# Expert weights in three steps: when a duo's gate, up and down transfers begin

## The reference

```
hid = silu(xe @ e_gate) * (xe @ e_up)      # e_gate, e_up: 1024 x 2816 each
ye  = hid @ e_down * gate                  # e_down: 2816 x 1024
```

## Time and profile before

| | us |
|---|---|
| median of 3 runs (3658.36 to 3662.4) | 3662.31 |
| profiled execution | 3664.57 |
| its span, first to last instruction | 3662.8 |
| TensorE busy (matmul rows) | 3345.7 (91%) |
| VectorE busy | 2133.3 (58%) |
| DMA: 670.98 MB over the span | 183 GB/s on average |

### The profile page before, as it was taken

One profiled execution on the slowest core, in us unless ns is written; L12 is line 12 of the kernel. 1 busy time (PEld: TensorE's weight loads), 2 busy tenths in 40 slices (PEclk: granted clock), 3 DMA queues, 4 the chain that ended last, 5 costly groups with the idle time before them and its releaser, 6 DMA issues.

```text
span 3662.8 us, 154096 instructions
## 1 busy us (share of the span) xinstructions
PE 3345.7 (91%) x72354; PEld 2883.5 (79%) x72354; DVE 2133.3 (58%) x3890; ACT 764.4 (21%) x1815; POOL 384.6 (10%) x536
## 2 busy tenths in 40 slices
PE   7989898998999986699999999999999999999998
PEld 3575767666555543599999999999999999999997
DVE  3567566665344445556566566565656565665655
ACT  3434344443344432000000000000000000000002
POOL 0142415243211000000000000000001000000001
PEclk9999999999999987799999999999999999999999
DMA  8200000000311131878778777777778777877775
GB/s 348 70 5 9 18 9 17 10 14 4 101 32 26 42 110 58 304 258 282 264 276 276 267 280 264 275 271 267 267 268 281 263 270 271 284 269 266 270 269 191
DMA packets 500361, 670.98 MB, mean 183 GB/s; under 512 B 31598, under 2 KB 438406, under 8 KB 496654
## 3 DMA queue, kind: packets, MB, share of 16 engines
q1 hardware_dynamic: 494030, 641.74, 49.8%
q0 software_dynamic: 5520, 19.34, 2.5%
q10 hardware_dynamic: 176, 0.05, 0.0%
HBM read 631.68 MB, written 28.30 MB: 180 GB/s over the span
## 4 chain that ended last, share of the span: by engine, by line
PE 56%; issue 3%; DVE 0%; DMA 0%; ACT 0%; DVEq 0%; POOLq 0%
PE banks L2508 34%; PE banks L2533 20%; PE banks L2449 2%; DMA e_xe<-scratch_h2d,idx 0%; DVE e_wgu L2812 0%; DVE e_wgu L2881 0%; DVE e_xe L2870 0%; DVE e_wsum L2720 0%; DVE e_wsum L2725 0%; DVE e_wgu L2715 0%; ACT e_xp L2648 0%; ACT e_xT L2648 0%; DVE e_wsum L2710 0%; DVE e_ye L2783 0%; DVE e_xpT L2729 0%
## 5 line engine op out<-in xcount | busy, mean ns | idle before, releaser
L2533 PE MATMUL banks<-e_hid,e_wd 128*64 128x144 f32 x11264 | 1273.1, 287 | 21.2 <-issue 18.1
L2533 PEld LDWEIGHTS banks<-e_hid,e_wd 128*64 128x64 f32 x11264 | 768.5, 137 | 32.9 <-issue 32.5
L2508 PE MATMUL banks<-e_xsum,e_wgu 128*64 128x72 f32 x11264 | 524.6, 227 | 32.2 <-issue 31.7
L2508 PE MATMUL banks<-e_xsum,e_wsum 128*64 128x72 f32 x11264 | 525.9, 227 | 25.9 <-issue 23.8
L2508 PEld LDWEIGHTS banks<-e_xsum,e_wgu 128*64 128x64 f32 x11264 | 499.4, 138 | 36.4 <-issue 35.8
L2508 PEld LDWEIGHTS banks<-e_xsum,e_wsum 128*64 128x64 f32 x11264 | 501.3, 137 | 31.3 <-issue 29.0
L2508 PE MATMUL banks<-e_xT,e_wgu 128*64 128x72 f32 x11264 | 515.5, 227 | 10.7 <-issue 10.5
L2743 DVE TENSOR_TENSOR e_gu<-e_first,banks 128x288 f32<-128x288 f32 x176 | 80.0, 455 | 762.3 <-ACT e_first L2629 565.3
L2508 PEld LDWEIGHTS banks<-e_xT,e_wgu 128*64 128x64 f32 x11264 | 496.6, 137 | 13.6 <-issue 13.6
L2629 ACT ACTIVATE e_first<-banks 128x144 f32<-128x144 f32 x176 | 51.1, 290 | 1518.7 <-PE banks L2508 1518.7
L2508 PE MATMUL banks<-e_xT,e_wsum 128*64 128x72 f32 x5632 | 263.0, 227 | 22.7 <-issue 22.3
(11 more groups left out here) (401 smaller groups left out, 4750.1 us busy)
## 6 DMA issues: line engine op xcount, KB each, us to landing
e_wgu<-in_e_gate SPq DMA_DIRECT2D x176, 1024.0 KB, 5.4
e_wgu<-in_e_up SPq DMA_DIRECT2D x176, 1024.0 KB, 8.7
e_wd<-in_e_down SPq DMA_DIRECT2D x176, 1024.0 KB
h_wmod<-in_w_mod SPq DMA_DIRECT2D x24, 1024.0 KB, 15.3
wblk<-in_w_in SPq DMA_DIRECT2D x22, 512.0 KB, 21.7
h_x<-in_x_sample SPq DMA_DIRECT2D x8, 512.0 KB, 6.9
wo<-in_w_out SPq DMA_DIRECT2D x2, 2048.0 KB, 12.0
scratch_ffn<-hT_x SPq DMA_DIRECT2D x8, 512.0 KB, 5.1
```

The source lines that it names most:

```text
L2508: last = nc.tensor.matmul(bank[4 + 2 * (n % 2) + g][c, q * HT:(q + 1) * HT], a[:, k, c], b[:, k, :], start=(k == 0), stop=(k == HALF - 1))
L2533: last = nc.tensor.matmul(bank[k // PER_BANK][c, at:at + TOK], wd[n % WD][:, b, k * P + h * CH:k * P + (h + 1) * CH], hid[n % 2][:, b, :], ...
```

## The change

A second semaphore, `products_done` (`pace` in the code), is raised by each of the first thirteen products of a duo; the fourteenth raises `gu_ps` as before. SyncE no longer waits on `gu_ps` in the loop. It begins the gate transfer of duo n after the first product of duo n - 3, the up transfer after the sixth, and the down transfer after the tenth (and, as before, after `used` allows it). The slots, sizes and order of the transfers stay, and the first four duos are loaded without waiting for the gate and up slots, as before.

```diff
--- before.py
+++ after.py
@@ -2303,7 +2303,7 @@
         bank = K.bank
         g_in = [sem(f"gate_up_in{i}") for i in range(WG)]
         d_in = [sem(f"down_in{i}") for i in range(WD)]
-        used = sem("duo_used")
+        used, pace = sem("duo_used"), sem("products_done")
         rows = sem("gt2_in")
         x_in, xh_ps, x_ps, xa_ok, xv_ok, xs_ok = (sem(n) for n in ("x_in", "xT_half_psum", "xT_psum", "xT_act", "xT_dve", "x_sums"))
         ts_ok, ws_ok, wsum_ok = sem("token_chain"), sem("weight_chain"), sem("weight_sums")
@@ -2355,9 +2355,13 @@
                     e, j = divmod(n, ND)
                     f = slice(j * DUO * P, (j + 1) * DUO * P)
                     if n >= WG:
-                        sp.wait_ge(gu_ps, n - WG + 1)
+                        sp.wait_ge(pace, (STEPS - 1) * (n - WG + 1) + 1)
                     sp.dma_start(wgu[n % WG][:, 0, :, :], gv[:, e, :, f]).then_inc(g_in[n % WG], 16)
+                    if n >= WG:
+                        sp.wait_ge(pace, (STEPS - 1) * (n - WG + 1) + 6)
                     sp.dma_start(wgu[n % WG][:, 1, :, :], uv[:, e, :, f]).then_inc(g_in[n % WG], 16)
+                    if n >= WG:
+                        sp.wait_ge(pace, (STEPS - 1) * (n - WG + 1) + 10)
                     if n >= WD:
                         sp.wait_ge(used, n - WD + 1)
                     sp.dma_start(wd[n % WD][:, :, :], dv[:, e, j * DUO:(j + 1) * DUO, :]).then_inc(d_in[n % WD], 16)
@@ -2594,13 +2598,13 @@
                             pe.wait_ge(wsum_ok, n + 1)
                         last = product(n, 0, q)
                         if mats(n) == 2:
+                            last.then_inc(pace, 1)
                             done = downs(done, STEPS * n + 2 * q)
                             last = product(n, 1, q)
                         else:
                             for i in range(2 * KD * q // QS, 2 * KD * (q + 1) // QS):
                                 last = up(n, i)
-                        if q == QS - 1:
-                            last.then_inc(gu_ps, 1)
+                        last.then_inc(gu_ps if q == QS - 1 else pace, 1)
                         done = downs(done, STEPS * n + 2 * q + 1)
                         if n and q == 3:
                             between(*divmod(n - 1, ND))
```

## The result

| | before | after |
|---|---|---|
| median of 4 runs each | 3660.34 us | 3577.72 us (3574.02 to 3581.53) |
| ratio | | 0.9776, 95% interval 0.9759 to 0.9793 |
| profiled execution | 3664.57 us | 3574.02 us |
| its span | 3662.8 us | 3572.3 us |

The change makes the kernel 2.2% faster. The prediction said 3629 us, 0.9%, with a range from 3588: the direction and the bound hold, the gain is two and a half times as large.

A forecast was written before the change was run, and what follows sets the result against it. TensorE bounds the kernel, idle 0.765 us per duo at block borders where instruction packets wait behind weights. Waits and increments 0, idle time -33.5 us: 3664.57 to 3631, 3629 us on the median's scale; range 3588 to 3672.

The forecast's parts named there:

- the SyncE waits: SyncE, per duo: one wait on gu_ps becomes three on products_done; nobody becomes late, cost 0.
- the increments: TensorE: thirteen more semaphore increments per duo, 2288 in all; taken as 0, bounds -23 to +23 us.
- rival (b): Block packets: their wait does not depend on how much is queued, so no change, 3655 to 3669 us; chance 0.12.
- two rules of the Trainium skill: Block crossings are "mostly hidden"; DMA engines go round queues packet by packet. By either, the change would win nothing.
- Three lone transfers: 3 x 0.19 = 0.57 us per duo in place of 0.765: TensorE's idle time at block borders: each separately begun transfer costs 0.19 us; gain 0.195 us per duo, 33.5 us.
- the triangle of the upper bound: Borders within 2.8 us of a start all wait for landing: 0.79 us per transfer, 2.4 per duo, +280 us.
- The lower bound of the same term: Lone transfer's idle time at least about 0.10 us, so 0.30 per duo and -80 us.
- "issue" waits near 90 us: Sign in the profile after: weight loads' steady-part waits near 90 us in place of 123, at the same 161 duos.
- a duo of 11.95 us: Sign in the profile after: a duo takes some 11.95 us; it took 12.17 before.
- the idle time is spread over the duo: Sign: idle time in three places of the duo, each 5 to 7.5 us after a transfer's start, none dominating.
- Rival (c): Block borders: nearly all idle time goes, w below 2.5 us for lone transfers; 3533 us at most, half 3590; chance 0.12.
- Rival (a): Block borders: each small transfer holds a block like a full queue; +60 us, about 3722, half-way 3690; chance 0.18.

The follow-up runs named there:

- the gate alone: Changed kernel without up transfers from the fifth duo and down transfers from the seventh, gate after product 1: 3522.05 us.
- the up-8 kernel: Changed kernel without down transfers from the seventh duo on, gate after product 1 and up after product 8: 3611.90 us.
- half a block behind the borders: Changed kernel with transfers cut into 0.5 MB halves, begun in groups 64 weight loads after TensorE's instruction block borders: 3709.05 us.

## Why the prediction was wrong

**What held.** The bound (TensorE stands at block borders, for instruction packets that wait behind weights): with no weights 370 crossings cost nothing, with all together after product 1 nearly everything is back (0.703 of 0.742). That nothing else moves: no wait of TensorE on a weight transfer appeared, the SyncE waits made nothing late, and the increments cost at most 2 ns. The places at which the transfers begin, 3 to 4 us apart, were right too. "No change", rival (b), for which two rules of the Trainium skill were brought up, is out as a forecast. Half of its mechanism is right, though: how long a packet waits hardly depends on how much is queued.

**The step that failed** is the term of the sum, "Three lone transfers: 3 x 0.19 = 0.57 us per duo in place of 0.765". A lone transfer measured 0.010 us and the three 0.291. The 0.19 was read from the stretch 4.5 to 7.5 us behind the gate's start, as "this is just that first part". It was not a lone transfer's situation, in three ways, which are read from the traces and not tested one by one:

- Most borders that made that stretch already stood behind up and down as well as gate, all three begun within 1.04 us. Borders 1 to 3 us behind a gate's start have 48.5 us of idle time after them in the kernel before (76 borders), and 1.3 us with the gate alone (60 borders). At b = 1.5 to 2 us the median w was 3.43 before and 2.74 after; above the free 2.5 us that is 0.9 against 0.2. In the table b counts from the last start, which before is mostly the down transfer, about 1 us behind the gate.
- I took the landing, 5.3 us, as the time until which a block waits. The packets start at 4.5 us. So the idle time of one border is at most 2.0 - b, not 2.8 - b; the triangle of the upper bound halves, from 2.8 x 2.8 to 2.0 x 2.0.
- History was left out. Before, a block came so late that the next border had no lead. A lone transfer is followed by a free border, which restores the lead, and a border within some 1.2 us of a start is then mostly safe. By an estimate from these figures this is the largest part: without it a lone transfer could still cost up to 2.0 x 2.0 / 2 / 4.94 = 0.40 us, with it up to 0.8 x 0.8 / 2 / 4.94 = 0.06 us; measured are 0.010.

The lower bound of the same term, 0.10 us per lone transfer or 0.30 per duo, -80 us, was what came out (0.291; 82.6 us). That is luck: the bound had 0.10 for each of three lone transfers, and what was measured is 0.010 for a lone one and nearly all of the 0.291 from the three disturbing each other, a term that the sum does not have. The bound was also left just outside the stated range, whose low end of 3588 us stood 10 us above the measured time. Step by step: "issue" waits near 90 us were 48.6; a duo of 11.95 us was 11.68; the idle time is spread over the duo, the early part the largest (0.13).

Rival (c), with a chance of 0.12, came nearest. The time lies between its 3533 and its half-way point, and its mechanism is what the gate alone shows: w stays below 2.5 us behind a lone transfer at 346 of 370 borders, and at a border in the first microsecond the packet does go ahead of the data (0.1 to 0.2 us). The prediction set it aside for the 0.19. It does not hold for the three together, whose packets still stand behind the weights. Half of its gain is, by the way, 3664.57 - 66 = 3599 us, not 3590.

Rival (a), slower, was a real danger though not here: its point, 0.255 us per start, is reached by the up-8 kernel (0.513 for two), and half a block behind the borders its 60 us nearly came (3709 us, 51 above the kernel before beside it).

## What to carry to other kernels

Where a long unrolled program shows short "issue" idle times at a fixed number of instructions, look at the instruction queue beside the data queues: bulk transfers begun together can hold up the program's own blocks, and spreading them in time cost nothing here, where their data had time to spare. Do not take a stretch of a full queue as the price of a lone transfer: measure the lone one, by leaving the others out. And the place of a start against the blocks can be worth more than its distance from other transfers, so try neighbouring places before trusting one: without the down transfers, moving the up transfer from product 8 to 10 or 6 took away 0.35 and 0.43 us of idle time per duo, 60 and 75 us in all, while moving all three starts of the change by one or two products moved nothing.

## What the runs showed of the hardware

- A 16 KB block of TensorE's program, 128 weight loads with their matmuls, is in time if its packet starts within 2.5 to 2.7 us of the border before it; each further us is a us of idle time (w of 4.05, 4.07 and 4.2 us: idle 1.57, 1.58 and 1.52). Without weights its median start is 0.13 us behind the border, and it costs nothing.
- With no weights ahead, the packet starts 1.1 us earlier when the block before came in time (0.1 to 0.2 us against 1.1 to 1.3 behind the border). That this is the sequencer's lead is my reading of it; no run takes the lead away by itself.
- A lone transfer of 1 MB holds a packet until 4.5 us behind its start. With three queued, which take 10.5 us to land, 99% of the packets still start within 4.5 us of their border. Halves of 0.5 MB begun every 2 us land after 5.0 us each.
- Two megabytes queued at once and the third alone cost nearly as much as all three at once (0.66 and 0.70 us of idle time per duo).
